# Seven block products instead of eight in the up projections of two MLPs

## The reference, cut to what matters

```python
x = x + jnp.concatenate([mix, mem_out], axis=-1) @ p['w_out'][l]
h2 = rmsnorm(x, p['norm2'][l])
x = x + jnp.square(jax.nn.relu(h2 @ p['w_mlp1'][l])) @ p['w_mlp2'][l]
```

## Time and profile before

| | |
|---|---|
| three timed runs | 1274.8, 1275.93, 1279.19 us; median 1275.93 |
| the profiled execution | 1271.49 us, span 1269.5 us |
| PE, PEld busy | 96%, 92% |
| DVE, ACT, POOL busy | 45%, 32%, 27% |
| chain of waits that ended last | PE 90%, of it L445 81% |

### The profile page before, as it was taken

How to read it: one execution, slowest core, us unless ns; L and a number is a source line. 1 busy time by engine, 2 the same in 40 slices (tenths; PEclk the granted TensorE clock), 3 DMA queues, 4 the chain that set the end, 5 groups by cost and what they waited for, 6 DMA issues and landing times.

```text
span 1269.5 us, 23370 instructions
## 1 busy us (share of the span) xinstructions
PE 1217.5 (96%) x9674; PEld 1169.8 (92%) x9674; DVE 572.0 (45%) x856; ACT 408.7 (32%) x756; POOL 346.5 (27%) x284
## 2 busy tenths in 40 slices
PE   6998999999999999999999999699999999999997
PEld 5877999999999999998899766599999999999997
DVE  7667544333333333356634766645333333333334
ACT  7445342212212212344422366533212222212221
POOL 3363024205305305320054200013401511511521
PEclk9999999999999999999999999899999999999998
DMA  7624422232232222232345357023222232232222
GB/s 279 216 86 119 130 84 83 88 96 84 84 92 87 88 86 85 88 93 84 135 120 133 133 200 243 1 67 98 86 84 84 88 96 84 84 100 84 84 67 71
DMA packets 38033, 132.98 MB, mean 105 GB/s; under 512 B 4178, under 2 KB 7122, under 8 KB 37298
## 3 DMA queue, kind: packets, MB, share of 16 engines
q1 hardware_dynamic: 36834, 123.42, 31.3%
q0 software_dynamic: 1104, 8.15, 2.1%
HBM read 121.18 MB, written 7.03 MB: 101 GB/s over the span
## 4 chain that ended last, share of the span: by engine, by line
PE 90%; DVE 6%; ACT 2%; issue 1%; DMA 0%; POOL 0%; DVEq 0%; SPq 0%; ACTq 0%
PE psum L445 81%; DVE weights_split L1085 1%; DVE inv_rms L1104 1%; PE psum L622 1%; PE psum L545 1%; ACT weights_split L809 1%; PE psum L548 1%; PE psum L531 1%; PE psum L558 1%; PE psum L604 1%; PE psum L578 0%; PE psum L584 0%; PE psum L562 0%; DVE tiny L1189 0%; PE psum L490 0%
## 5 line engine op out<-in xcount | busy, mean ns | idle before, releaser
L445 PE MATMUL psum<-operand_b,weights_split 128*128 128x272 f32 x4416 | 562.3, 289 | 4.1 <-DVE weights_split L1085 3.9
L445 PEld LDWEIGHTS psum<-operand_b,weights_split 128*128 128x128 f32 x4416 | 556.4, 189 | 9.0 <-DVE weights_split L1085 4.9
L445 PE MATMUL psum<-operand_a,weights_split 128*128 128x272 f32 (+1 forms) x4068 | 520.2, 289 | 22.3 <-DVE weights_split L1085 15.0
L445 PEld LDWEIGHTS psum<-operand_a,weights_split 128*128 128x128 f32 x4068 | 513.4, 190 | 28.5 <-issue 21.0
L809 ACT ACTIVATE weights_split<-weights_raw 128x1024 fp32r<-128x1024 f32 (+1 forms) x186 | 192.6, 1036 | 395.2 <-PE psum L445 395.2
L1085 DVE TENSOR_TENSOR weights_split<-weights_raw,weights_split 128x1024 fp32r<-128x1024 f32 (+1 forms) x186 | 239.4, 1287 | 136.6 <-ACT weights_split L809 136.5
L1505 POOL TENSOR_TENSOR squares<-staging 128x544 f32<-128x544 f32 x64 | 76.3, 1193 | 469.6 <-ACT operand_b L855 207.5
L1139 DVE TENSOR_TENSOR residual<-psum,residual 128x544 f32<-128x544 f32 x48 | 34.8, 725 | 175.9 <-PE psum L445 175.9
L1120 DVE SCALAR_TENSOR_TENSOR staging<-psum,inv_rms 128x544 f32<-128x544 f32 x56 | 40.6, 725 | 150.0 <-PE psum L445 150.0
L1498 POOL TENSOR_TENSOR squares_sum<-squares_sum,squares 128x544 f32<-128x544 f32 (+1 forms) x35 | 48.6, 1387 | 115.6 <-ACT squares L821 115.1
L1507 POOL TENSOR_TENSOR operand_a<-squares,operand_a 128x544 fp32r<-128x544 f32 x32 | 64.9, 2029 | 2.5
(11 more groups left out here) (210 smaller groups left out, 713.8 us busy)
## 6 DMA issues: line engine op xcount, KB each, us to landing
weights_raw<-in_weights SPq DMA_DIRECT2D x180, 512.0 KB, 3.6
cache_tiles<-in_page_k SPq DMA_DIRECT2D x16, 384.0 KB, 4.0
...
cache_tiles<-in_mem_k SPq DMA_DIRECT2D x8, 512.0 KB, 4.8
cache_tiles<-in_mem_v SPq DMA_DIRECT2D x8, 512.0 KB, 5.2
residual<-in_x SPq DMA_DIRECT2D x1, 2176.0 KB, 12.2
...
```

Of the source, the lines that this page charges most:

```text
L445: mm = pe.matmul(ps[:, 2 * (j % PS) + hf, 0:n], w(wr), act[:, ar, k, hf * n:(hf + 1) * n], start=(q == 0 and wr == 0 and ar == 0), stop=(q ...
```

## The change: seven block products for two up units

Two up units and their 1024 inner features are taken as a 2 x 2 block matrix: weights a11, a12 (unit u, first and second half of the inner dimension) and a21, a22 (unit u+1); tokens likewise by inner half and by column half (272 each). The four output blocks come from seven products of 4 slices x 3 = 12 matmuls of 272 columns, where the scheme before needs eight. Down units and all other units stay as they were.

- Weight sums, POOL (`up_weights`, four 128x512 operations a pair): s1 = a21 + a22, s2 = s1 - a11, then a11 - a21 in the place of a21, then a12 - s2 in the place of s2. s1 and s2 lie in `mem_keys` and `mem_values`, one place each for all pairs.
- Split of the seven weight blocks: `up_high` on ACT, `up_rest` on DVE, 128x512 each; six have a place each (`up_weights_a`, `up_weights_b`), refilled for the next pair while PE works at this one.
- Token blocks, once per MLP, in `out_units`: three further blocks (t2, t3, t4) from the gained residual, which is now also multiplied by the inverse rms of the norm before (`inv_rms`); the new `rms_up` undoes that in `inverse`.
- Outputs, DVE (`up_phase`): seven additions of 272 columns from PSUM to `up_partial` or `staging`, then relu and scaling in place in `staging`. A pair fills four banks; two pairs alternate.
- The square for POOL is made by ACT in place in `staging`; POOL is left with the subtraction.
- One group of cache loads moves on SP from ahead of `U_OUT0`'s loads to the last down phase of the first MLP, since `mixed_tokens` lies in that memory.

```diff
# PE
+ for q in range(7):
+     pe.wait_ge(up_lo, ...) if q < SUMS else pe.wait_ge(weight_lo, u + 2)
+     if q == 0: pe.wait_ge(unit_out, u - 2 if p else u - 1)
+     if q == 1 and p == 0: pe.wait_ge(unit_out, u)
+     if q == 4: pe.wait_ge(up_copied, pair + 1)
+     if q == 5: pe.wait_ge(up_read, 2 * pair + 1)
+     if q == 6: pe.wait_ge(up_read, 2 * pair + 2)
+     for kk in range(KQ): for wr, ar in ((0, 0), (0, 1), (1, 0)): pe.matmul(...)   # 272 columns
# DVE, out_units, second half of the residual tiles
-                    norm_rest(g, j, X[:, j, :], pair_of(dst, j))
-                    rest(u0 + j + HL)
+    own.chain(dve.scalar_tensor_tensor(out=at, in0=X[:, k, :], scalar=gain(g, k), in1=rms[:, :], ...))
+    own.chain(dve.tensor_tensor(t3, at[:, HALF:TOK], T[:, kk, HALF:TOK], ALU.subtract))
+    own.chain(dve.tensor_tensor(t2, t3, T[:, kk, 0:HALF], ALU.add))
+    dve.tensor_tensor(t4, at[:, 0:HALF], t2, ALU.subtract).then_inc(tok_raw, 1)
+    if k + HL < KT: rest(u0 + k + HL)
+    dve.wait_ge(tok_hi, KQ * l + kk + 1)
+    dve.tensor_tensor(mixed_tokens[:, :, 1, kk, :], ...).then_inc(tok_lo, 1)
# ACT, residual_tokens
+    square(r, k, X[:, k, :], TOK)
+    act.wait_ge(tok_raw, ...)
+    act.activation(mixed_tokens[:, :, 0, k - KQ, :], ...).then_inc(tok_hi, 1)
+    act.activation(dst[:, 0, k, :], raw_tokens[:, k, :], ACT.Copy).then_inc(norm_hi, 1)
+    # behind residual_tokens: high(u + k + HL)
# DVE, up_phase, one pair
+    if p: second(p - 1)        # one addition, relu and scaling of the pair's second tile
+    up_rest(u0, i, b, p, 6); up_rest(u0, i, b, p + 1, 0); up_rest(u0, i, b, p + 1, 1)
+    s16 = bank B + s1;  s165 = bank C + s16  -> up_read
+    up_rest(u0, i, b, p + 1, 2)
+    s16 = bank D + s16;  t2 = bank D + s165  -> up_read
+    up_rest(u0, i, b, p + 1, 3);  t1 = bank A + s1
+    up_rest(u0, i, b, p + 1, 4);  t1 = bank C + s165
+    if first and p == 0: inverse(r)
+    t1 = max(t1, 0) * rms -> unit_out;  up_rest(u0, i, b, p + 1, 5)
# POOL
-                pool.tensor_tensor(sq, t, t, ALU.mult).then_inc(hid_sq, 1)
+    up_weights(u0, i, b, p + 1, (0, 1));  hidden_rest x 2;  up_weights(u0, i, b, p + 1, (2, 3))
+    # s2 waits for up_rest 5 of the pair before; a12 - s2 waits for up_rest 2 of its own pair
```

More of the change, by code:

```diff
@@ L52 @@
 BLOCKS = 4
+PAIRS = KT // 2
+KQ = KT // 2
+SUMS = 6
+BANK_A, BANK_B, BANK_C, BANK_D = range(4)
+UP_BANK = (BANK_A, BANK_C, BANK_B, BANK_D, BANK_A, BANK_C, BANK_D)
 RAW, HL, PS, TS = 4, 2, 2, 4
@@ L293, in unit_psum, with up_bank, up_split, up_source @@
             return ps[:, 2 * (j % PS):2 * (j % PS) + 2, 0:HALF]
+        def up_bank(p, bank):
+            return ps[:, 4 * (p % 2) + bank, 0:HALF]
+        def up_split(q):
+            if q < 4:
+                return up_a[:, q]
+            if q < SUMS:
+                return up_b[:, q - 4]
+            return split[:, 1, 0, :].rearrange("p (r c) -> p r c", r=2)
+        def up_source(q, s):
+            s1, s2 = memKT[:, 0].rearrange("p a b -> p (a b)"), memVt[:, 0].rearrange("p a b -> p (a b)")
+            return (raw[:, s, 0:D // 2], s1, s2, raw[:, s + 1, 0:D // 2], raw[:, s, D // 2:D], s2,
+                    raw[:, s + 1, D // 2:D])[q]
+        def up_tokens(h2, q, r, kk):
+            first, second = slice(0, HALF), slice(HALF, TOK)
+            if q in (0, 1):
+                return h2[:, r, kk, first if q == 0 else second]
+            if q in (4, 5):
+                return h2[:, r, KQ + kk, first if q == 4 else second]
+            return mixed_tokens[:, {2: 0, 3: 1, 6: 2}[q], r, kk, :]
+        def raw_turn(i, u):
+            return i * 64 + 16 * (u // RAW + 1)
         chunks = ([("mem", 0, c) for c in range(4)] + [("mem", 1, c) for c in range(4)]
@@ L427, in _, with unit @@
         def _(pe):
[L428 removed]
+            def unit(u, j, act, kts=tuple(range(KT)), cols=TOK, ready=None, base_kt=0, first=False, mid=None, late=None, held=PS - 1):
                 pe.wait_ge(weight_lo, u + 1)
                 if not first:
[L433 removed]
+                    pe.wait_ge(unit_out, u - held)
                 n = cols // 2 if cols == TOK else cols
@@ L501, in block_ @@
                 def block_(i, u, first, last=False):
-                    for j in range(KT):
-                        unit(u + j, u0 + j, h2, ready=normed(g) if first and j == 0 else None)
-                        if first and j == 0:
-                            norm_sum(r)
+                    for p in range(PAIRS):
+                        up_pair(u + 2 * p, p, PAIRS * (i + BLOCKS * (r == R_MLP1)) + p, first)
                     for j in range(KT):
@@ new lines, in mlp, with down_high, hidden_high, up_phase @@
+            def mlp(u0, hidden, r, nr, gs):
+                h0 = BLOCKS * PAIRS * (u0 == U_MLP1)
+                def down_high(i, b, j):
+                    u = b * 2 * KT + u0 + KT + j
+                    if j:
+                        weight_high(i * 2 * KT + u, u % RAW, raw_turn(i, u))
+                    else:
+                        act.wait_ge(raw_loaded[u % RAW], raw_turn(i, u))
+                        act.wait_ge(unit_done, i * 2 * KT + (u - KT))
+                        act.activation(split[:, 0, 0, :], raw[:, u % RAW, :], ACT.Copy).then_inc(weight_hi, 1)
+                def hidden_high(i, b, j):
+                    act.wait_ge(unit_out, i * 2 * KT + (b * 2 * KT + u0 + j + 1))
+                    act.activation(hidden[:, 0, j, :], T[:, j % TS, :], ACT.Square)
+                    act.activation(T[:, j % TS, :], T[:, j % TS, :], ACT.Square).then_inc(hid_hi, 1)
+                def up_phase(i, b, first=False):
+                    for p in range(PAIRS):
+                        pair = i * PAIRS + (h0 + b * PAIRS + p)
+                        if p:
+                            hidden_high(i, b, 2 * p - 2)
+                        up_high(u0, i, b, p, 6)
+                        if first and p == 0:
+                            act.wait_ge(sq_summed, (KT - 1) * (r + 1))
+                        act.wait_ge(up_done, pair * SUMS + 1)
+                        act.activation(up_part[:, p % 2, 0, :], up_bank(p, BANK_A), ACT.Copy).then_inc(up_copied, 1)
+                        if p < PAIRS - 1:
+                            up_high(u0, i, b, p + 1, 0)
+                        else:
+                            down_high(i, b, 0)
+                        if p:
+                            hidden_high(i, b, 2 * p - 1)
+                        for q in range(1, SUMS if p < PAIRS - 1 else 1):
+                            if first and p == 0 and q == 3:
+                                root(r)
+                            up_high(u0, i, b, p + 1, q)
+                    hidden_high(i, b, KT - 2)
+                    down_high(i, b, 1)
+                    hidden_high(i, b, KT - 1)
+                up_phase(0, 0, True)
@@ L1103, in inverse @@
                 t = rms_mem[:, :] if r == R_MEM else rms[:, :]
+                if r in (R_MLP0, R_MLP1):
+                    own.chain(dve.tensor_tensor(t, std[:, :], t, ALU.mult))
                 dve.reciprocal(t, t).then_inc(rms_ready, 1)
```

342 lines of the change are left out of this document (281 added, 61 removed).

## The result

The changed kernel took 1326.63 us, median of four runs (1324.89 to 1329.65), against 1275.37 us for the kernel before on the same chip: ratio 1.0402, 95% interval 1.0387 to 1.0417. Five more runs in a later series gave 1330.17, ratio 1.0394 (1.0366 to 1.0421). The direction was as forecast, and the cause in kind; the size was not: +20 forecast, +51 measured. The profiled execution has a span of 1322.7 us, 53.2 more than before. From the page of the changed kernel, to be set beside rows 1: busy times, and the granted clock in 40 slices.

The account below looks back on a forecast made before the run. The count of matmuls on PE bounded the kernel. Steady blocks -5.4 and first blocks +12.2 and +13.6 gave +20.4 on the profiled 1271.5, 1291.9; with 4.4 for the timed median, 1296 us, range 1256 to 1314.

Parts of the forecast that it names:

- What is taken away: Up phases: a pair needs 84 matmuls instead of 96; 384 fewer in 32 pairs, at most 48.1 us won.
- Collisions: Up phases: DVE and POOL wait for each other's whole instruction when operands are in SBUF, together 12.0 us a pair.
- Rival A: Collisions hardly matter: DVE's pass 8.7 us, steady blocks PE-bound, -36 us for six, total 1249; chance 0.22.
- The pass: DVE's work on one pair of up units: 13.3 us, of which 8.7 own work and 4.6 waits for POOL.
- the prediction's own formula: Steady MLP block lasts 25.9 + 1.6 x pass, not under 42.1 us; forecast 47.2 against 48.1.
- The clock: PE's granted clock in the up phases was expected to stay as in a busy window, so no time was counted.
- The first blocks: First block of each MLP: `w_out` tiles make DVE late and the inverse rms lengthens pair 0's pass; +12.2 and +13.6 us.
- Small edits: Moved cache loads: nothing, at most 2 us; next weights through two slots: nothing, up to 1 us a pass if late.
- The first ones near 63: Sign to look for: the first up phase of each MLP near 63 us, a steady one near 47.
- Rival C: Sums block DVE in full or raw weights come late: pass 14.5 to 15, total 1310 to 1320 us; chance 0.10.
- -5.4: Six steady MLP blocks together, -0.9 us each, in us.
- +25.8: The first blocks of the two MLPs together, forecast as +12.2 and +13.6 us.

Follow-up runs that it names:

- e2: The changed kernel with no weight sums at all, raw halves of the weights being split in their place: 1267.8 us (ratio 0.994).
- e1: The changed kernel with a pair's four weight sums replaced by POOL additions of the same size that nobody reads: 1328.2 us (ratio 1.0424).
- e4: The changed kernel with ACT making the high part of the weights two units ahead before the token copies in `w_out`: 1317.6 us (ratio 1.0337).
- c3: The changed kernel without weight sums, with outputs joined in and scaled from PSUM, and ACT's high parts ahead of the copies in `w_out`: 1251.5 us (ratio 0.9804).
- e5: The changed kernel with the additions written back into PSUM, and relu and scaling reading from there: 1308.4 us (ratio 1.025).
- e6: The changed kernel with the product with std and the reciprocal for the MLPs' inverse rms left out: 1321.0 us (ratio 1.0339).
- c5: c1 with matmuls that nobody reads where PE waits, in the loop blocks and the first blocks: 1290.7 us (ratio 1.0116).
- c1: The changed kernel with outputs joined in and scaled from PSUM, and ACT's high parts ahead of the copies in `w_out`: 1297.2 us (ratio 1.0172).
- e8: The changed kernel with 24 and 13 matmuls that nobody reads where PE waits in pairs 1 and 2 of the loop blocks: 1329.9 us (ratio 1.0411).

## Why the prediction had the direction and missed the size

- **What is taken away, right.** A loop block bound by PE takes 90.34 us (e2) where before had 96.2: 5.9 us each, as 4 x 1.5 promises.
- **Collisions, right in kind.** DVE and POOL each wait for the whole of the other's instruction unless an operand lies in PSUM: 1.85 against 0.68 us. The Trainium skill (SBUF — State Buffer, Who interferes with whom) calls the pair of ports that the two share an exclusive lock and has a DVE instruction with two SBUF inputs contend with a GpSimd instruction that reads SBUF; the trace agrees. Rival A needed 0.68 throughout, and falls by the trace, and by e1 and e2.
- **The pass, 0.75 us short.** Forecast 13.3, measured 14.05. The forecast was 8.7 us of DVE's own work and 4.6 of waits (its list of waits adds up to 4.2 to 5.7, not to the 4.5 to 5.2 given); the own work was 8.3 and the waits 5.8. The wait that the hand-made pass did not have is that of rest 1, 1.1 us: the instructions settle into an alternation in which relu and three rests pay 1.0 to 1.2 each, one behind the other. By the prediction's own formula (25.9 + 1.6 x pass) that is +1.2 a block; the rest of the undisturbed block's 97.1 is +0.6.
- **The clock, wrong.** It was "no term of mine", argued from rows 3, where PE was busy for 14 of 24 us at 0.86 and 17.9 of 20 at 1.00. Those windows hide when within them PE stood still: here single waits of 1.75 to 3.0 us in an up phase 90% busy were followed by 0.57 to 0.71 over 4 us. It cost 4.5 us in three loop blocks.
- **The first blocks, the step that failed.** Forecast +12.2 and +13.6, measured +20.2 and +23.6; 18 of the 32.4 us missed. The step is the working of `w_out`'s tiles, by which DVE would enter pair 0's pass 14.4 us after PE would have ended `w_out` at the pace of before. It entered after 20.1 us in layer 0 (201.49) and 22.1 in layer 1 (920.44): 13.4 of the 18. The rest of the up phase, 51.1 instead of 48.8, is 2.3 in each layer. The 14.4 had 1.5 us in it for POOL's weight sums and nothing for its sum of squares. That sum was there before the change too, but beside a DVE with idle time. Now it collides with most tiles, 1.1 us each, tile 4 has one or two more collisions with the weight sums, and this chain is serial: DVE, ACT, DVE, PE. That it is the sum of squares is read from the trace: L1289 takes 1.57 us beside it, and 0.44 at 147.05, where it begins just ahead. With ACT's order changed (e4, c3) tiles 0 to 3 all take 6.0 us again, though POOL adds the squares as before: the collision costs most where ACT's weights wait behind it. Without weight sums (e2) DVE enters the pass only 1.2 and 1.4 us earlier. No run took the sum of squares from POOL.
- **What the parts are worth.** Layer 0's first block falls by 8.3 us without the sums (e2), 5.3 with ACT's order changed (e4), 3.1 with relu from PSUM (e5), 3.0 without the reciprocal (e6; 4.1 by the account above). The first three together make 119.4 - 16.7 = 102.7, and c3 has 102.4. That agreement is luck: by the table the three would give 62.6 and 40.0 us for the two parts, and c3 has 60.6 and 41.8. In layer 1 they make 106.3, c3 103.7. So each cause is real, but they are not quite separate.
- **Small edits, right.** Moving the cache loads and the order of raw weights show no wait of PE.
- **Numbers that came out by luck.** "The first ones near 63": the first up phases took 63.5 and 63.4 us, but the forecast's 63.2 counts from where PE would have ended `w_out` before, and so counted they took 71.2 and 73.2. Rival C had loop blocks of +1 to +2, and +1.5 was measured on average, but by a pass of 14.5 to 15 and without the clock; its total, 1310 to 1320, was too low as well.

The sum: -5.4 became +9 (pass and block +10, clock +4.5), +25.8 became +43.8. In the first blocks the low clock seems to cost little: in c5, where two waits there were filled, they were no shorter than in c1. The 8.85 us of `w_out`'s unit 6 cost nothing: in e8, where it ran in 6.28 us, unit 7 waited for DVE all the same and began 49.9 us after `w_out`'s start, as in the changed kernel.

The arithmetic of c5 shows where such a scheme could still win: six loop blocks of 94.2 instead of 96.2 are -12 us, its first blocks +28. A version that keeps the eight products in the first block of each MLP, and makes the token blocks beside them, might keep the first and lose most of the second; it was not built, so that is open.
